# Linear-attention gate of a two-layer hybrid block: tokens down the partitions, applied to the read-out before its transposes

## The reference, cut to what matters

```python
proj = h @ w_in                       # h: 256 x 1024; columns q, k, v, ..., g_a, g_b
y_a = _dsa_attention(q, k, v, ...)    # softmax attention over picked keys
o_b = _gated_delta_rule(bq, bk, bv, g, beta)          # linear attention, 8 heads of 128, chunks
y_b = _rms_norm(o_b, gdn_norm).reshape(B, S, B_V)     # norm over the 128 features of a head
y = jax.nn.sigmoid(g_a) * y_a + jax.nn.sigmoid(g_b) * y_b
return y @ w_out
```

## Time and profile before

| | us |
|---|---|
| three runs of the kernel | 1096.40, 1095.16, 1097.67 (median 1096.4) |
| the profiled execution | 1096.33 |
| its span on the core, first to last instruction | 1094.5 |
| PE busy in the span | 1084.0 |
| POOL, DVE, ACT busy | 676.8, 614.5, 562.6 |

### The profile page before, as it was taken

The page is one execution under the profiler, slowest core; times in us unless marked ns, Lnnn a source line. Parts: engine busy times, 40 slices in busy tenths (PEclk is TensorE's granted clock), DMA queues, the critical chain, the costliest instruction groups (busy, mean ns, idle before and its releaser), DMA issues.

```text
span 1094.5 us, 18878 instructions
## 1 busy us (share of the span) xinstructions
PE 1084.0 (99%) x7585; PEld 983.7 (90%) x7586; DVE 614.5 (56%) x1116; ACT 562.6 (51%) x888; POOL 676.8 (62%) x359
## 2 busy tenths in 40 slices
PE   8999999999999999999999999999999999999997
PEld 7999999998898988888999999999988979888886
DVE  6789579355514652446458876783644345323454
ACT  7645864434645644444464567634355554444443
POOL 4886758627674457754477858685378444686442
PEclk9999999999999999999999999999999999999999
DMA  7544545624643655655555545546255345555553
GB/s 292 174 155 136 182 137 164 174 80 158 193 158 126 211 181 187 191 189 181 188 175 171 163 138 165 153 156 159 75 192 193 96 174 184 185 189 191 184 185 112
DMA packets 63333, 183.31 MB, mean 167 GB/s; under 512 B 18576, under 2 KB 19088, under 8 KB 63248
## 3 DMA queue, kind: packets, MB, share of 16 engines
q1 hardware_dynamic: 47936, 172.48, 49.1%
q10 hardware_dynamic: 15312, 9.64, 3.2%
HBM read 179.47 MB, written 2.62 MB: 166 GB/s over the span
## 4 chain that ended last, share of the span: by engine, by line
PE 96%; DMA 1%; ACT 1%; DVE 1%; issue 0%; POOL 0%; SPq 0%; DVEq 0%; ACTq 0%; POOLq 0%
PE psum L521 22%; PE psum L522 21%; PE psum L523 21%; PE psum L550 12%; PE psum L551 6%; PE psum L695 1%; PE psum L1021 1%; PE psum L1000 1%; DMA sb_raw<-weights 1%; PE psum L735 1%; PE psum L1122 1%; PE psum L915 1%; PE psum L908 1%; PE psum L790 1%; PE psum L625 1%; PE psum L718 1%
## 5 line engine op out<-in xcount | busy, mean ns | idle before, releaser
L418 POOL TENSOR_TENSOR sb_low<-sb_raw,sb_high 128x1024 fp32r<-128x1024 f32 x257 | 618.1, 2419 | 326.0 <-ACT sb_high L408 311.3
L408 ACT ACTIVATE sb_high<-sb_raw 128x1024 fp32r<-128x1024 f32 x322 | 340.1, 1061 | 390.2 <-DMA sb_raw<-weights 351.2
L521 PE MATMUL psum<-sb_h_both,sb_high 128*128 128x256 f32 x1096 | 311.4, 284 | 0.1
L523 PE MATMUL psum<-sb_h_both,sb_low 128*128 128x256 f32 x1096 | 309.5, 282 | 0.0
L522 PE MATMUL psum<-sb_h_both,sb_high 128*128 128x256 f32 x1096 | 308.8, 282 | 0.0
L521 PEld LDWEIGHTS psum<-sb_h_both,sb_high 128*128 128x128 f32 x1096 | 207.1, 189 | 1.5 <-issue 0.7
L522 PEld LDWEIGHTS psum<-sb_h_both,sb_high 128*128 128x128 f32 x1096 | 206.5, 188 | 0.2
L523 PEld LDWEIGHTS psum<-sb_h_both,sb_low 128*128 128x128 f32 x1096 | 205.7, 188 | 0.0
L550 PE MATMUL psum<-sb_h_both,sb_high 128*128 128x512 f32 x544 | 192.0, 394 | 0.0
L551 PE MATMUL psum<-sb_h_both,sb_low 128*128 128x256 f32 x544 | 152.1, 280 | 0.0
L418 DVE TENSOR_TENSOR sb_low<-sb_raw,sb_high 128x1024 fp32r<-128x1024 f32 x65 | 95.3, 1466 | 81.2 <-ACT sb_high L408 80.9
(11 more groups left out here) (313 smaller groups left out, 1700.4 us busy)
## 6 DMA issues: line engine op xcount, KB each, us to landing
sb_raw<-weights SPq DMA_DIRECT2D x322, 512.0 KB, 3.5
sb_pre_gain<-pre_gains ACTq DMA_DIRECT2D x6, 512.0 KB, 4.7
sb_post_gain<-post_gains ACTq DMA_DIRECT2D x6, 512.0 KB, 4.3
sb_kx<-mem SPq DMA_DIRECT2D x2, 512.0 KB, 4.6
sb_x<-x SPq DMA_DIRECT2D x1, 1024.0 KB, 10.8
t_dram<-sb_sq ACTq DMA_DIRECT2D x4, 256.0 KB, 3.2
out<-sb_x SPq DMA_DIRECT2D x4, 256.0 KB, 2.1
m_dram<-sb_m ACTq DMA_DIRECT2D x8, 64.0 KB, 2.1
```

What stands on the lines that cost most here:

```text
L408: nc.scalar.activation(high[:, n % HIGHS, :], raw[:, n % RAWS, :], ACT.Copy).then_inc(high_ready, 1)
L418: eng.tensor_tensor(low[:, k, :], raw[:, k, :], high[:, n % HIGHS, :].bitcast(F32), ALU.subtract).then_inc(low_ready[k], 1)
L521: pe.matmul(out, a[0], b[0], start=start, stop=False, **kw)
L523: return pe.matmul(out, a[1], b[0], start=False, stop=stop, **kw)
```

## The change

The columns g_b are laid out and multiplied in the tall form: 24 matmuls of 512 columns per slot, into banks 1 and 3 for slots 0 and 1 and banks 2 and 4 for slots 2 and 3. ACT makes both tanh of a pair after slots 1 and 3, in place of one after each slot, and writes them to the same memory, with tokens down the partitions. DVE multiplies the read-out by 1 + tanh in `o_norm`, before the transposes; the gate operation after them goes. The banks of att, v_tok and k_tok are named by hand. The order of `o_norm` becomes 0, 2, 1, 3, and a half slot of values moves between yb 1 and yb 2.

```diff
--- before.py
+++ after.py
@@ -265,6 +265,7 @@
         kT = kd_t[:, :].rearrange("p (g t) -> p g t", g=KV_HEADS)
         v_tok = v_t[:, :].rearrange("p (c d) -> p c d", c=TILES)
         sel_bias = selb_t[:, :].rearrange("p (c s) -> p c s", c=TILES)
+        gate_tok = gates_t[:, 2048:4096].rearrange("p (g n) -> p g n", g=4)
         qx = gates_t[:, 0:2048].rearrange("p (k t) -> p k t", t=S)
         px = gates_t[:, 2048:4096].rearrange("p (c h s) -> p c h s", c=TILES, h=X_HEADS)
         pxt = decay_t[:, :].rearrange("p (b h t) -> p b h t", b=TILES, h=X_HEADS)
@@ -786,7 +787,7 @@
                     for j in range(HEADS // 2):
                         what = ("att", j)
                         grp_kv = 2 * j // (HEADS // KV_HEADS)
-                        o = claim(what, (dve_att, what), beside)
+                        o = claim(what, (dve_att, what), ((2, 4, 0, 2)[j],), False)
                         pe.matmul(o, v_tok[:, 0, grp_kv * DH:(grp_kv + 1) * DH], pt0[:, 2 * j:2 * j + 2, :],
                                   start=True, stop=False, skip_group_check=True)
                         o2 = o.rearrange("p (h t) -> p h t", h=2)
@@ -795,12 +796,14 @@
                         mm.then_inc(pe_att.sem, mark(pe_att, what))
 
                 for g in range(4):
-                    wide(("gb", g), h, (act_gate, ("gb", g)), beside)
+                    if g % 2 == 0:
+                        gate_banks = [claim(("gb", c, g // 2), (act_gate, ("gb", c, g // 2)), (((1, 3), (2, 4))[g // 2][c],), False) for c in range(TILES)]
+                    tall("gb", g, h, gate_banks)
                     if g == 0:
                         attended()
                     c, hh = g // 2, g % 2
                     what = ("v_tok", g)
-                    o = claim(what, (dve_gdn, what), beside)
+                    o = claim(what, (dve_gdn, what), ((4, 0, 3, 3)[g],), False)
                     if g == 0:
                         pe.wait_ge(*dve_conv.at(layer, ("silu", 11)))
                     for i in range(4):
@@ -808,11 +811,12 @@
                     tr.then_inc(pe_gdn.sem, mark(pe_gdn, what))
                 for hh in range(2):
                     what = ("k_tok", hh)
-                    o = claim(what, (dve_gdn, what), ((4, 0)[hh],), hh == 0)
+                    o = claim(what, (dve_gdn, what), (1 - hh,), False)
                     for i in range(4):
                         tr = pe.transpose(o[:, i * P:(i + 1) * P], conv[:, 4 * hh + i, 0:P], ident)
                     tr.then_inc(pe_gdn.sem, mark(pe_gdn, what))
 
+                turn[0] = 5
                 pe.wait_ge(low_loaded, 16 * BLOCKS * (layer + 1))
                 steps_done, memory_at = [0], [None, None]
                 memory_keys = ([("xk", 2, 1)] if layer == 0 else []) + both("xk", 3)
@@ -960,6 +964,8 @@
                 values(0, (0,) if layer == 0 else (0, 1))
 
                 for j in range(G_HEADS // 2):
+                    if j == 2:
+                        values(*((0, (1,)) if layer == 0 else (1, (0,))))
                     what = ("yb", j)
                     o = claim(what, (dve_part, ("y_low", j)), ((4, 2, 5, 3)[j],))
                     if j % 2 == 0:
@@ -973,8 +979,7 @@
                     tr.then_inc(pe_gdn.sem, mark(pe_gdn, what))
 
                 if layer == 0:
-                    values(0, (1,))
-                values(1, (0,))
+                    values(1, (0,))
 
                 y_half = lambda part, half: [claim((part, c, half), (dve_norm, ("x", part, c)), (4 + 2 * c + half,)) for c in range(TILES)]
                 y_banks = lambda part: [y_half(part, half) for half in range(2)]
@@ -1526,7 +1531,12 @@
                     gate("ga", i, 0)
 
                 for i in range(4):
-                    gate("gb", i, 8)
+                    high_parts(ahead(("gb", i), 3))
+                    act.wait_ge(*slots.at(layer, ("gb", i)))
+                    if i % 2 == 1:
+                        for c in range(TILES):
+                            nc.scalar.activation(gate_tok[:, 2 * c + i // 2, :], bank(("gb", c, i // 2)), ACT.Tanh, scale=0.5)\
+                                .then_inc(act_gate.sem, act_gate.mark(("gb", c, i // 2)))
                     if i == 0:
                         act.wait_ge(*dve_gdn.at(layer, "t_block"))
                         nc.scalar.activation(t_block_low, t_psum.rearrange("p j i -> p i j"), ACT.Copy).then_inc(act_gdn.sem, act_gdn.mark("t_block_low"))
@@ -2213,7 +2223,11 @@
                 def o_norm(g):
                     c, hh = g // 2, g % 2
                     dve.wait_ge(*pool_gdn.at(layer, ("o_scale", g)))
-                    V.tensor_tensor(o_tok[:, g, :, :], bank(("o", g)).rearrange("p (h n) -> p h n", h=4), cols(oscale[:, c, 4 * hh:4 * hh + 4], P), ALU.mult)\
+                    o = bank(("o", g))
+                    by_heads = o.rearrange("p (h n) -> p h n", h=4)
+                    link(V.tensor_tensor(by_heads, by_heads, cols(oscale[:, c, 4 * hh:4 * hh + 4], P), ALU.mult), dve_gdn, ("o_scaled", g))
+                    dve.wait_ge(*act_gate.at(layer, ("gb", c, hh)))
+                    V.scalar_tensor_tensor(out=flat(o_tok[:, g, :, :]), in0=gate_tok[:, g, :], scalar=1.0, in1=o, op0=ALU.add, op1=ALU.mult)\
                         .then_inc(dve_gdn.sem, dve_gdn.mark(("o_norm", g)))
 
                 o_mean(1)
@@ -2224,7 +2238,7 @@
                 o_norm(0)
                 for g in (2, 3):
                     o_mean(g)
-                for g in (1, 2, 3):
+                for g in (2, 1, 3):
                     o_norm(g)
 
 
@@ -2236,10 +2250,7 @@
                 for j in range(G_HEADS // 2):
                     low_parts(ahead(("yb", j), 2))
                     dve.wait_ge(*pe_gdn.at(layer, ("yb", j)))
-                    dve.wait_ge(*act_gate.at(layer, ("gb", j)))
                     o = bank(("yb", j))
-                    link(V.scalar_tensor_tensor(out=o, in0=flat(gates[:, 8 + 2 * j:10 + 2 * j, :]), scalar=1.0,
-                                                in1=o, op0=ALU.add, op1=ALU.mult), dve_gdn, ("yb", j))
                     V.scalar_tensor_tensor(out=o, in0=o, scalar=half_gdn, in1=flat(y[:, 2 * j:2 * j + 2, :]), op0=ALU.mult, op1=ALU.add)\
                         .then_inc(dve_gdn.sem, dve_gdn.mark(("y", j)))
                     if j % 2 == 1:
@@ -2361,10 +2372,10 @@
         w_in = w["w_in"][layer]
         part = lambda name: w_in[:, COL[name]:COL[name] + SIZES[name]]
         tokenwise = np.concatenate([part("iw"), part("ba"), part("bb")], 1)
-        mats = {**{k: part(k) for k in ("iq", "k", "q", "bq", "bk", "bv", "ga", "gb")},
+        mats = {**{k: part(k) for k in ("iq", "k", "q", "bq", "bk", "bv", "ga")},
                 "xk": w["w_xkv"][layer][:, 0:D], "xq": w["w_xq"][layer],
                 "gate": w["w_gu"][layer][:, 0:FF], "up": w["w_gu"][layer][:, FF:]}
-        tall = {"out": w["w_out"][layer], "xo": w["w_xo"][layer], "xv": w["w_xkv"][layer][:, D:]}
+        tall = {"gb": part("gb"), "out": w["w_out"][layer], "xo": w["w_xo"][layer], "xv": w["w_xkv"][layer][:, D:]}
         for n, (at, name, i, b) in enumerate(ORDER):
             if at + (name == "nk") != layer:
                 continue
```

## The result

| | before | after |
|---|---|---|
| executions beside each other, us | 1095.01, 1095.16, 1096.40, 1097.67 | 1098.65, 1110.31, 1110.69, 1110.80 |
| median, us | 1095.78 | 1110.50 |
| the profiled execution: time, span | 1096.33, 1094.5 | 1110.31, 1108.6 |

After over before is 1.0103, with a 95% interval of 1.0079 to 1.0126: slower, and 11.6 us above the forecast of 1098.9. Three executions of four have a mean granted clock of 0.986 or 0.987. The fourth has 0.998 and took 1098.65, which is where the forecast was.

The account below looks back on a forecast made before the run. The prediction took PE as the bound: its start-to-start distances plus its waits. Shorter matmuls and new waits summed to +1.17 us in the first layer and +1.36 in the second, +2.5 on 1096.40: 1098.9 us, range 1097.2 to 1100.8.

Parts of the forecast that it names:

- S = +1.15: First layer, first memory-key matmul: PE's shift against the kernel before, negative for earlier; forecast 1.15 us later after waiting for a tanh.
- The sum: Both layers: 1.17 us in the first and 1.36 in the second, together +2.5 us.
- The tanh: First layer, memory keys in bank 2: PE waits for a tanh after gb 3, 1.7 us.
- My bound: First layer, wait for the tanh: with a varying landing, PE's shift S there is +0.1 to +1.5 us.
- Att 3, second layer: Att 3 in bank 2 waits for DVE's read of att 0: 1.42 us, against 0.18 in the first layer.
- for its two ends are both in the trace: Second layer, att 3: reason given for bounding its wait between 1.3 and 1.5 us.
- The matmuls: gb slots: 48 wide matmuls become 24 tall ones, gaining 0.14 us a slot, 1.1 us over 8 slots.
- so nothing gives this back: Whole kernel: PE's later work depends on its earlier work, which releases its weights, so the +2.5 us stays.
- Keys, yb and `out` of the second layer: Second layer: PE waits 0.20 us at the memory keys, 0.09 at yb 0 and 0.20 at `out`.
- The matmuls did not save what their durations say: Rival on the gb matmuls, chance 0.03: recorded durations save 4.1 us a slot, 33 in all, about 1066 us.
- the banks did bite: Rival, chance 0.05, claimed the opposite: both bank waits absent, 1095.6 us, no measurable change.
- no place behind the norm was 0.4 late: Rival, chance 0.10: each of four places at yb and `out` 0.4 us later, 1.6 us more, 1100.5 us.

## Why the prediction was wrong

**The step that failed** is "PE starts at 220.25 with the same 0.10 ... S = +1.15". It counted a wait of PE as its length. It said nothing on what PE's clock does in a pause in front of small blocks, and no rival had it, although show 40 slices of full clock only for a kernel in which PE never waits a full microsecond, but for 1.5 us at its very start. The runs with the pause put into the old form, those that fill it and those that take it away show that the 11.5 us between the two groups are this. The Trainium skill (TensorE: Matmul & The Clock Gate, section "HAM oscillation — how this bites in real kernels") says that waits between bursts of matmuls make the clock drop to half rate, so that what comes behind runs cold; the traces agree, at 0.50. The waits it describes there, of some 3 to 5 us, are longer than the pauses of 2.17 to 2.68 us behind which the clock fell here. The sum put this cost of a wait at nothing, and gave no reason.

**Right, by the executions without the fall.** Four of the twelve have a median of 1099.02 against the forecast 1098.9. That closeness is partly luck, since terms were off in opposite directions (the tanh and the lost gain one way, att 3 the other):

- *The tanh.* Forecast a wait of 1.7 us; it was 2.41 and 2.17. The mechanism was right to the row: high part, tanh, key block. The landing came late, 219.29 for the high part where the forecast had 218.92 - 0.31 = 218.61. My bound let S go up to +1.5, by no row; it was 220.93 - 219.10 = +1.83 and, in the second trace, +1.87. The one row behind it bounded only an earlier landing.
- *Att 3, second layer.* Forecast 1.42; 0.06 and 0.17 in the two traces of the kernel after (in the first layer 0.06 and 0.49, forecast 0.18). The bank does make PE wait for DVE's first read, as the 0.72 in the run with the values moved back shows (gather 4.65), and 0.57, 0.56 and 0.54 in those with 4 fillers, with the longer wait and with fillers behind the wait (gather 4.48, 4.44 and 4.26). What was wrong is "for its two ends are both in the trace". One of them hung on a DRAM gather: from its issue to DVE's start it took 5.14 us in the execution I read (707.07 to 712.21), 5.41 and 5.43 in the two others of the old form, but 3.96 to 4.65 in seven of the new form, and in the eighth, with 12 fillers in the wait, it had landed when DVE came 3.77 behind the issue. I bounded a landing by rows of one execution, of the kernel without the change. Why it comes sooner in the new form is open.
- *The matmuls.* Right: from one v_tok to the next PE takes 6.06 us in the kernel after (205.17 to 211.23) where it took 6.19 (205.30 to 211.49), so a slot gains 0.13, forecast 0.14. Without the wait, `out` of the first layer starts at 260.17 against 260.81, 0.64 sooner, though not by the matmuls alone: at the keys it was 0.31 (218.79 against 219.10), and the other half, up to yb, is not traced to its cause. But "PE's later work depends on PE's earlier work ... so nothing gives this back" was wrong for the gain. In that kernel PE stands at the low part of a weight half soon after:

```profile
291.92 0.50 PE L522 MATMUL psum<-sb_high,sb_mem_high 128*128 128x512 f32 x1 [0.66 <-DVE sb_low L419]
```

The same matmul started at 291.73 before, so -0.64 became +0.19. DVE's conversion stands behind ACT's, ACT's behind the weights' transfers, and these did not move. This is read from the trace and was not tested; it says where much of the 1.1 us of shorter matmuls may have gone in a kernel that comes out at 1.0002.
- *Keys, yb and `out` of the second layer.* 0.20, 0.09, 0.20 forecast; 0.20, 0.13, 0.28 measured.
- *Rivals.* The matmuls did not save what their durations say, the banks did bite (the keys' by 2.41 us, att 3's by 0.06 to 0.72), no place behind the norm was 0.4 late. The kernel is slower, as forecast, but by 14.7 us at the median where 2.5 were forecast; the range ended at 1100.8.

**What stays open.** Why one execution falls and the next does not. In the table longer pauses do not fall reliably more often, and with these counts 3 of 10 and 8 of 12 can't be told apart for certain; the rows come from runs on different chips besides. Nor is the end of the pause the moment of the fall: it came 0.2, 0.6 and 1.8 us after PE's restart in the three traces with small blocks behind, and 0.3 us before it with the fillers. Whether the landing of the very execution or something outside the kernel decides it is not shown, since only one execution of each run has a trace.

## What to carry to other kernels

Count a wait of PE twice: by its length, and by what stands behind it. If small blocks follow, a pause of some 2 us can cost, on top of itself, five times its length, and in a share of the executions only, so that a median of few can land on either side. That small blocks are what makes it costly is likely, not settled. Where an in-order engine makes both the thing PE needs now and a conversion for later that waits on a transfer, put the first in front: here one call moved past two tanh was worth 14 us in two executions of three. Where a wait can't be removed, unread dense matmuls that fill it kept the clock in 7 executions of 7, at 0.4 us over the executions that wait and don't fall (1099.44 against 1099.02); a third of the fillers were not enough in 4 of 12.

## What the runs showed of the hardware

- The granted clock fell to 0.50 behind pauses of 2.17, 2.35, 2.41 and 2.68 us in the profiled executions, and did not behind pauses of 1.62, 2.28 and 2.88. Of the two groups of executions this makes, the medians are 11.5 us apart in the kernel after.
- With the 32- and 64-wide blocks and the 256-column steps between them behind the pause, and PE busy throughout, the clock stayed at 0.50 for 27.3 us in each of three traces (221.2 to 248.5, 222.8 to 250.1, 762.6 to 789.9), 2.6 to 5.3 us beyond the last small block; with 12 dense matmuls of 512 columns it was back after 3.4 (221.4 to 224.8).
- In one trace the clock fell only after PE had worked for 1.8 us at full clock behind the pause.
- A DRAM gather of 64 x 1024 floats took 3.96 to 5.43 us from its issue to its reader in ten profiled executions, for the same code at the same place: the three of the old form 5.14 and more, the seven of the new one 4.65 and less. Why is open.
